# Level products of two scan directions in all quadrants, and an output projection on high and low parts

## What is computed

```python
def wkv7_scan(S0, inputs, reverse):
...
    def step(S, inp):
        r, w, k, v, kk, a = inp
        S = (S * w[:, :, None, :]
             - jnp.einsum('bhvk,bhk->bhv', S, kk)[..., None] * (kk * a)[:, :, None, :]
             + v[..., None] * k[:, :, None, :])
        return S, jnp.einsum('bhvk,bhk->bhv', S, r)
...
def odd_mixer(h_lat, h_ctx, cos, sin, w_in, w_out, sink, ctx_out):
...
    o_lat, o_ctx = window_gqa(apply_rope(q_l, cos, sin), apply_rope(k_l, cos, sin), v_l,
                              q_c, k_c, v_c, sink, ctx_out)
    return o_lat @ w_out, (o_ctx @ w_out if ctx_out else None)
```

## Time and profile before

| | |
|---|---|
| median of three runs | 2604.84 us (2599.87 to 2604.89) |
| the profiled execution | 2601.52 us, its span 2599.7 us |
| mean granted TensorE clock | 0.978 of full speed |
| TensorE, matmuls | 2442.0 us, 94% of the span |
| TensorE, loads of weights | 1989.0 us, 77% |
| VectorE | 1454.3 us, 56% |
| ScalarE | 875.5 us, 34% |
| GpSimd | 76.5 us, 3% |
| HBM, read | 307 MB, 119 GB/s over the span |
| scan | from 1099 to 1364 us |
| tail and second output projection | from 2325 to 2385 us |

### The profile page before, as it was taken

One profiled execution on the slowest core, in us unless ns is written; L12 is line 12 of the kernel. 1 busy time (PEld: TensorE's weight loads), 2 busy tenths in 40 slices (PEclk: granted clock), 3 DMA queues, 4 the chain that ended last, 5 costly groups with the idle time before them and its releaser, 6 DMA issues.

```text
span 2599.7 us, 41895 instructions
## 1 busy us (share of the span) xinstructions
PE 2442.0 (94%) x17718; PEld 1989.0 (77%) x17718; DVE 1454.3 (56%) x2326; ACT 875.5 (34%) x1491; POOL 76.5 (3%) x148
## 2 busy tenths in 40 slices
PE   8999999999999999678887999999999999999998
PEld 6687778688887767567875788877688877777997
DVE  5555565655554578666544555545655554563553
ACT  2341132422222435532224422222422222454543
POOL 0000000000000000000000000000000000000000
PEclk9999999999999999798989999999999999999999
DMA  8236526344434310000003344444344433202553
GB/s 299 99 115 218 185 98 210 138 146 135 140 138 146 132 65 33 1 3 4 4 3 130 107 144 139 137 140 145 129 138 145 136 144 125 93 33 84 190 180 130
DMA packets 55913, 310.91 MB, mean 120 GB/s; under 512 B 5936, under 2 KB 9392, under 8 KB 28080
## 3 DMA queue, kind: packets, MB, share of 16 engines
q1 hardware_dynamic: 32944, 224.75, 24.3%
q0 software_dynamic: 20736, 75.51, 8.8%
q10 hardware_dynamic: 2048, 7.98, 0.8%
HBM read 307.16 MB, written 1.05 MB: 119 GB/s over the span
## 4 chain that ended last, share of the span: by engine, by line
PEld 42%; PE 30%; issue 12%; DVE 10%; ACT 5%; PEldq 0%; DMA 0%; DVEq 0%; SPq 0%; ACTq 0%
PEld bank L1410 14%; PEld bank L1403 13%; PEld bank L1406 12%; PE bank L1252 5%; PE bank L1461 4%; PE bank L1249 2%; PE bank L1311 2%; PE bank L1327 2%; PE bank L1067 1%; PE bank L1074 1%; PE bank L1070 1%; PE bank L1139 1%; PE bank L983 1%; ACT hn L1832 1%; DVE ms L2293 1%
## 5 line engine op out<-in xcount | busy, mean ns | idle before, releaser
L2306 DVE TENSOR_TENSOR w_lo<-ring,w_hi 128x1024 fp32r<-128x1024 f32 (+1 forms) x195 | 232.5, 1192 | 441.1 <-ACT w_hi L1795 441.1
L1403 PE MATMUL bank<-ffn_x_hi,w_hi 128*128 128x512 f32 x984 | 388.7, 395 | 0.0
L1406 PE MATMUL bank<-ffn_x_lo,w_hi 128*128 128x512 f32 x984 | 388.7, 395 | 0.0
L1410 PE MATMUL bank<-ffn_x_hi,w_lo 128*128 128x512 f32 x984 | 388.7, 395 | 0.0
L1795 ACT ACTIVATE w_hi<-ring 128x1024 fp32r<-128x1024 f32 (+1 forms) x195 | 200.5, 1028 | 282.0 <-PE bank L1406 271.0
L2235 DVE SCALAR_TENSOR_TENSOR ms<-mod_rows,c_silu 128x1024 f32<-128x1024 f32 x200 | 244.0, 1220 | 1.3
L1403 PEld LDWEIGHTS bank<-ffn_x_hi,w_hi 128*128 128x128 f32 x984 | 184.4, 187 | 45.2
L1406 PEld LDWEIGHTS bank<-ffn_x_lo,w_hi 128*128 128x128 f32 x984 | 184.4, 187 | 45.2
L1410 PEld LDWEIGHTS bank<-ffn_x_hi,w_lo 128*128 128x128 f32 x984 | 184.4, 187 | 45.0
L1403 PE MATMUL bank<-ffn_h_hi,w_hi 128*128 128x512 f32 x528 | 213.4, 404 | 0.0
L1410 PE MATMUL bank<-ffn_h_hi,w_lo 128*128 128x512 f32 x528 | 208.6, 395 | 0.0
(11 more groups left out here) (456 smaller groups left out, 4580.6 us busy)
## 6 DMA issues: line engine op xcount, KB each, us to landing
ring<-in_stream SPq DMA_DIRECT2D x211, 1024.0 KB, 4.8
mod_rows<-in_mod_stream POOLq DMA_DIRECT2D x144, 512.0 KB, 3.8
one_const<-in_one ACTq DMA_DIRECT2D x1, 1665.0 KB, 14.5
mix_const<-in_two ACTq DMA_DIRECT2D x1, 1440.0 KB, 6.6
win_const<-in_win ACTq DMA_DIRECT2D x1, 1216.0 KB, 5.2
x<-in_x SPq DMA_DIRECT2D x4, 256.0 KB, 4.7
c_silu<-in_c SPq DMA_DIRECT2D x1, 1024.0 KB, 10.3
x<-in_x SPq DMA_DIRECT2D x1, 1024.0 KB, 26.8
```

The lines of the kernel that those rows point to most:

```text
L1403: mm = pe.matmul(bank[:, 0:tok], w_high, hi, start=k == 0, stop=False)
L1406: mm = pe.matmul(bank[:, 0:tok], w_high, lo, start=False, stop=False)
L1410: mm = pe.matmul(bank[:, 0:tok], w_low, hi, start=False, stop=last)
L2306: V.tensor_tensor(low[:, 0:h.nk, :], raw_half(h), high[:, 0:h.nk, :].bitcast(F32), ALU.subtract).then_inc(sem("w_split"), 1)
```

## The change

**Levels.** An inverse level is no longer two steps but single products, each of one direction: `inner` (b x m), `inverse` (mt x t1, which updates m) and `transposed` (t1 x mt, which updates mt). `inner` of one direction is issued matmul by matmul in turns with a product of the other direction: inner of direction 0 with the inverse product of direction 1 from the level before, inner of direction 1 with the inverse product of direction 0 (in the fifth level with its transposed one). The transposed products are alone, except that one. In direction 1 the matrix N has its chunks swapped between the partition halves (`swapped`), so that its two products write, or read, the other half than direction 0's: the pair stands in four quadrants of the array. A level has four steps: inner of direction 0, transposed product of direction 1 from the level before, inner of direction 1, transposed product of direction 0. The signal `level_ready` becomes two, `m_ready` and `mt_ready`, and VectorE's subtractions (`update`) wait for one bank each. A round has 9 such pairs and 10 single products.

**First products.** So that both layouts are there, the k = 0 step takes three banks (`near`, `pair`, `far`) and has five matmuls for each (g, c) in place of four; ScalarE copies for direction 1 both N transposed and its swapped form (`nt_for_b`) in one instruction, and both halves of k = 0 now stand before the first u.

**Late work.** The 30 late pieces are spread over `LATE_OVER` = 54 steps, and `OUT_FROM` moves with the number of steps from 68 to 95.

**Second projection.** `project` is dropped; `project_parts` takes the layer, with four buffers for weight parts in the second. The splits of the first four half tiles stand behind pairs 10, 11, 13 and 14 of `blend(1)`, the split of input part c behind the pair that `OUT_PARTS_AFTER` names. ScalarE's evictions of the tail signal `came_out`, which it waits for before it splits their result.

```diff
-LATE_FROM, OUT_FROM = 3, 68
+LATE_FROM, LATE_OVER, OUT_FROM = 3, 54, 95
...
-    s["project"]("w_out_2o", 1, SEQ)
+    s["project_parts"](1, SEQ)
...
+OUT_SPLIT_AFTER = 10, 11, 13, 14
+OUT_PARTS_AFTER = 13, 13, 14, 14, 15, 16, 18, 18
...
+                if layer:
+                    for n in range(4):
+                        if OUT_SPLIT_AFTER[n] == i:
+                            yield "out_weight", n
+                    for c in range(KC):
+                        if OUT_PARTS_AFTER[c] == i:
+                            yield "out_parts", c
...
+OUT_SLOTS = SPLITS, 4
...
+            return lambda n: (ph4["w_hi"][:, (n + SPLITS) % 4], ph4["w_lo"][:, (n + SPLITS) % 4])
...
+        scan[0]["nt"] = scan[0]["nt_for_b"] = idle.pop(0)
+        scan[1]["nt"], scan[1]["nt_for_b"] = rs2[:, 0, :], rs2[:, 1, :]
...
-                    for what in ("inner", "outer"):
-                        yield (what, i, lvl)
+                    yield ("inner", i, lvl, 0)
+                    if lvl > 1:
+                        yield ("outer", i, lvl - 1, 1)
+                    yield ("inner", i, lvl, 1)
+                    if lvl < LEVELS - 1:
+                        yield ("outer", i, lvl, 0)
+                yield ("outer", i, LEVELS - 1, 1)
...
+        def beside_inner(lvl, d):
+
+            if d == 0:
+                return ("inverse", 1, lvl - 1) if lvl > 1 else None
+            return ("inverse", 0, lvl) if lvl < LEVELS - 1 else ("transposed", 0, lvl)
...
-                    yield late[k - LATE_FROM]
+                while late and k >= LATE_FROM + (before - len(late)) * LATE_OVER // before:
+                    yield late.pop(0)
...
+                def small(product, h, c):
+
+
+                    bank, lhs, rhs, swapped, part = product
+                    r, col = by_head(c), by_head(h)
+                    return pe.matmul(part(bank[by_head(c ^ swapped), col]), lhs[r, col], part(rhs[r, col]), start=True, stop=True)
...
+                def product_of(kind, i, d, lvl, bank):
+
+                    way, mt = scan[d], scan[d]["mt"][i % 2]
+                    if kind == "inner":
+                        return bank, way["b"], way["m"], d, lambda t: t
+                    if kind == "inverse":
+                        return bank, mt, way["t1"], d, lambda t: blocks(t, lvl, d)
+                    return bank, way["t1"], mt, 0, lambda t: blocks(t, lvl, 1 - d)
...
+                def wait_for_outer(i, d, lvl):
+                    pe.wait_ge(sem(f"inner_ready{d}"), (LEVELS - 1) * i + lvl)
+                    pe.wait_ge(sem(f"mt_ready{d}"), LEVELS * i + lvl)
...
-                        for d in range(2):
+                        lvl, d = more
+                        beside = beside_inner(lvl, d)
+                        if beside:
+                            kind, e, at_lvl = beside
                             bank, full = take_bank()
-                            pe.wait_ge(sem(f"level_ready{d}"), LEVELS * i + lvl)
-                            small(bank, scan[d]["b"], scan[d]["m"]).then_inc(full, 1)
+                            wait_for_outer(i, e, at_lvl)
+                            second, second_full = product_of(kind, i, e, at_lvl, bank), full
+                        bank, full = take_bank()
+                        pe.wait_ge(sem(f"m_ready{d}"), (LEVELS - 1) * i + lvl)
+                        own = product_of("inner", i, d, lvl, bank)
+                        for h in range(8):
+                            for c in range(2):
+                                mm = small(own, h, c)
+                                if (h, c) == (7, 1):
+                                    mm.then_inc(full, 1)
+                                if beside:
+                                    mm = small(second, h, c)
+                                    if (h, c) == (7, 1):
+                                        mm.then_inc(second_full, 1)
...
-                        lvl, = more
-                        for d in range(2):
-                            way, mt = scan[d], scan[d]["mt"][i % 2]
-                            bank, full = take_bank()
-                            pe.wait_ge(sem(f"inner_ready{d}"), (LEVELS - 1) * i + lvl)
-                            if lvl < LEVELS - 1:
-                                small(bank, mt, way["t1"], lambda t: blocks(t, lvl, d))
-                            small(bank, way["t1"], mt, lambda t: blocks(t, lvl, 1 - d)).then_inc(full, 1)
+                        lvl, d = more
+                        bank, full = take_bank()
+                        wait_for_outer(i, d, lvl)
...
+                        if k == 0:
+                            near, pair, far = (take_bank() for _ in range(3))
+                            for g in range(4):
+                                for c in range(2):
+                                    rows = [by_head(nth ^ d) for d in range(2)]
+                                    cols = [slice(pairs[d] * P + c * C, pairs[d] * P + (c + 1) * C) for d in range(2)]
+                                    bt, kt = ([scan[d][name][rows[d], g, cols[d]] for d in range(2)] for name in ("bt", "kt"))
+                                    here, there, left, right = by_head(c), by_head(1 - c), by_head(g), by_head(4 + g)
+                                    groups = ((near, here, left, bt[0], kt[0]), (pair, here, left, bt[1], kt[1]),
+                                              (near, here, right, kt[0], bt[0]), (pair, there, right, bt[1], kt[1]),
+                                              (far, there, left, kt[1], bt[1]))
+                                    for (bank, full), to, at, lhs, rhs in groups:
+                                        mm = pe.matmul(bank[to, at], lhs, rhs, start=True, stop=True)
+                                        if (g, c) == (3, 1) and not (to is here and at is left):
+                                            mm.then_inc(full, 1)
...
+            def out_weight(layer, n):
+                if n == 0:
+                    out_used[0] = tally("w_used", KC - 1)
+                split_high(parts_out[layer], n, out_used[0], out_half(layer), 0, OUT_SLOTS[layer])
+
+            def out_high(layer, kc, tok):
+                o = (ph4 if layer else ph2)["o"]
+                nc.scalar.activation(mixed[layer]["x_hi"][:, kc, 0:tok], o[:, kc, 0:tok], ACT.Copy).then_inc(sem("o_hi_ready"), 1)
...
+            def project_parts(layer, tok):
...
                 for c in range(KC):
+                    if OUT_SLOTS[layer] <= c + OUT_SLOTS[layer] - 1 < KC:
+                        out_weight(layer, c + OUT_SLOTS[layer] - 1)
...
+                    elif what == "out_weight":
+                        out_weight(1, i)
+                    elif what == "out_parts":
+                        act.wait_ge(sem("came_out"), 2 * i + 2)
+                        out_high(1, i, SEQ)
...
+                        if u.bufs is ph4:
+                            wait_read(free)
+                            act.nop().then_inc(sem("came_out"), 1)
...
+                        if d == 0:
+                            nc.scalar.activation(way["nt"][:, cols], bank[:, 0:256], ACT.Copy).then_inc(sem("nt_ready0"), 1)
+                        else:
+                            pair = bank[:, :].rearrange("p (n t) -> p n t", n=2)
+                            nc.scalar.activation(rs2[:, :, cols], pair, ACT.Copy).then_inc(free, 1)
+                            wait_read(free)
+                            act.nop().then_inc(sem("nt_ready1"), 1)
+                            turns.next()
...
+            def out_low(layer, kc, tok):
+                if kc == 0:
+                    out_base[0] = tally("o_hi_ready", KC)
+                dve.wait_ge(sem("o_hi_ready"), out_base[0] + kc + 1)
+                o, to = (ph4 if layer else ph2)["o"], mixed[layer]
+                V.tensor_tensor(to["x_lo"][:, kc, 0:tok], o[:, kc, 0:tok], to["x_hi"][:, kc, 0:tok].bitcast(F32),
+                                ALU.subtract).then_inc(sem("o_split"), 1)
...
                 for c in range(KC):
+                    if OUT_SLOTS[layer] <= c + OUT_SLOTS[layer] - 1 < KC:
+                        split_low(parts_out[layer], c + OUT_SLOTS[layer] - 1, out_half(layer))
...
+                def update(i, kind, d, lvl):
+
+                    inverse = kind == "inverse"
+                    parity = d if inverse else 1 - d
+                    part = blocks(scan[d]["m"] if inverse else scan[d]["mt"][i % 2], lvl, parity)
+                    bank, free = full_bank()
+                    link(V.tensor_tensor(part, part, blocks(bank[:, :], lvl, parity), ALU.subtract))
+                    dve.nop().then_inc(free, 1)
+                    dve.nop().then_inc(sem(f"m_ready{d}" if inverse else f"mt_ready{d}"), 1)
...
-                                V.tensor_tensor(eight(b), eight(nt), wkv_mask(d, 1), ALU.mult)
+                                V.tensor_tensor(eight(b), eight(way["nt_for_b"]), wkv_mask(d, 1), ALU.mult)
...
 
...
```

(7 more changed lines are left out.)

178 lines of the change are left out of this document (70 added, 108 removed).

## The result

The changed kernel takes 2609.59 us in the median of 14 runs (2601.31 to 2614.58), the one before 2603.80 in 14 runs beside them. The ratio is 1.0026, 95% interval 1.0019 to 1.0032: 5 to 8 us slower. The forecast was 2583, with a range of 2568 to 2601, and 0.82 on faster. The profiled execution has a span of 2607.3 us, 7.6 more than before.

What follows compares the result with a forecast made beforehand. It took TensorE to bound the scan's levels and VectorE the head of each round, with VectorE the longer chain after the change. Scan -24.5 and projection with tail +3.8 gave -20.7 us, hence 2583 us, range 2568 to 2601.

Steps and rivals of the forecast that it cites:

- The array: Scan levels: two products on disjoint quadrants take about 0.95 us together, saving 8.6 us a round, 34 us in all.
- Rival 3: Level products: a pair does not overlap in the array; +12 to +16 us, 2618 us; chance 0.06.
- First products: Scan, k = 0 step: 1.84 us a half in place of 0.93, +1.8 us of TensorE a round, hidden in round 2.
- So the levels are TensorE's: Scan, round 2: the five levels run without a gap on TensorE, 34.3 busy of 35.0 us, so TensorE bounds them.
- VectorE as the new bound: Scan after the change: VectorE is the longer chain, with 16 us of levels a round; round 2 takes 48 us.
- hand-overs: Scan, round 2: 3.5 us added to VectorE's chain, an estimate of about 0.2 us a step.
- Rival 2: Scan: VectorE takes back most of the gain, scan gives 10 us, tail takes 4; 2598 us (2592 to 2602); chance 0.25.
- By rounds: Scan, rounds 0 to 3: -1, -9, -9 and -5.5 us, together -24.5 us.
- The tail: End of the second mixer: four hoisted weight splits cost 2.35 us each, 9.4 in all; with input parts +10.3 us.
- The projection: Second projection: 26.1 us in place of 32.6, -6.5 us.
- The sum: Whole kernel: scan -24.5 us, projection and tail together +3.8 us, total -20.7 us.

Runs made afterwards that it cites:

- scan_only: The change to the scan alone, with the old second projection, against the kernel before: ratio 1.0003 (0.9994 to 1.0013).
- partner_wide: scan_only with the second product of each pair done by 8 matmuls of 128 columns, partly wrong weights: ratio 0.9956 to the kernel before.
- scan_nomask: scan_only with VectorE's masks of b behind level 1 replaced by ones of 8 columns, so b is wrong: ratio 0.9973 to the kernel before.
- out_early: The second projection's change alone, old scan, with the tail's splits moved to earlier pairs and VectorE's parts set separately: ratio 0.9997 to the kernel before.
- dense: The kernel before with one chunk product (k = 1, first pair of chunks) done eight times in one run of 256 matmuls: its 512 records took 14.0 us.
- after: The kernel with the whole change, against the kernel before: 2609.59 us, ratio 1.0026.
- pad_real: The kernel before with an empty instruction that raises an unread semaphore behind each matmul of every level product: 2775.68 us.
- pad: The kernel before with a plain empty instruction behind each matmul of every level product; these never reached the chip: ratio 0.9996.

## Why the prediction was wrong, by its own steps

- **The array: right.** A pair was to take 0.95 us; in the rows above it took 0.96. By the Trainium skill, page "TensorEngine Tiling (Array Packing)", section "Restrictions and Gotchas", its row tiles could not write one bank at the same time; this trace again shows otherwise, 64 records in 0.96 us on two banks. Rival 3 (pairs don't overlap) is out. The busy time saved was smaller than forecast all the same: the level products kept TensorE busy for 118.3 us and now for 93.5, so 24.8 less where 34 was forecast, and the scan as a whole has 14.5 less in place of some 27.
- **First products: right.** 1.84 us a half were forecast. In round 2 both halves, 160 records, ran from 1221.57 to 1224.80, 1.6 us each.
- **"So the levels are TensorE's": the step that failed.** I read 34.3 busy of 35.0 us as work of the array, and took 9 x 0.95 us a round off it, with nothing in the sum for bringing in the instructions. The number was right and the reading wrong. A single product's 64 instructions took 0.94 us, so 256 took 3.76, and the supply brought 256 in 3.4 us at best and in 3.9 where the new levels of round 2 waited for it: the old levels already ran at about that pace, and the array's speed was no longer what to save on. In round 2, 48 us were forecast; it took 60.3, with 10.7 us of waits put down to issue (3.1 before). The pairs take no instruction away, and the first products add 64 (32 records and their loads) a round. The sign was in rows that I had: 32 records at 14.4 ns in L1515 are 1.8 us for 128, a pace that blocks 3.3 us apart can't keep up, and L1515 has 3.5 us of issue in the waits of the kernel before. I had no rival for it.
- **VectorE as the new bound: not what bound first.** The rounds were summed along VectorE, with 3.5 us for hand-overs in round 2. In the levels of that round TensorE waited for VectorE not once. In the whole scan its waits ahead of level products are 13.2 us, 9.2 of which it had before. VectorE does come next: its masks are worth 8 us in scan_only, and its waits grow when instructions get fewer (partner_wide). Rival 2 let VectorE take back most of the gain and gave 2598; the measured time lies above its range as well, and its cause is another. Even with the instructions halved, the pairs did not beat the old order.
- **By rounds.** Forecast -1, -9, -9 and -5.5 us; the trace shows 0, -2.7, +4.3 and +0.3, and +1.3 behind the fourth round, where the granted clock is 0.73 for 0.77 before. The -2.7 of round 1 is no more than two traces of the unchanged scan differ by. In all, TensorE ran at half clock for 73 us of the scan in place of 63; what that cost no run tells apart, but in the levels of round 2 the clock was full from 1237.4 to 1274.9, so there it is not the reason.
- **The tail: right.** +10.3 us were forecast, though its terms as printed add up to 10.9. The first gated sum is 13.3 us later than before and the rotation at the head of the tail 2.7, so +10.6. Two pairs begin 4.5 us apart across a split in place of 2.46 (4.8 forecast): 2330.07 and 2334.59.
- **The projection: right.** From the first to the last gated sum it was 28.8 us and is 23.1, -5.8; forecast -6.5 for the whole.
- **The sum.** -24.5 should have been +3 by the trace and +0.9 (-1.5 to +3.4) by the timed runs; +3.8 for tail and projection was +4.8 by the trace, +7.0 (4 to 10) by the timed runs.

What stays open: how the loss splits between supply and VectorE outside the levels of round 2. partner_wide gives 12 us back and scan_nomask 8, and the two overlap by an amount that no run told apart. Nor was a kernel tried in which the pairs keep their length and every instruction, with neither limit in the way, so that the 8.6 us a round of the array were never seen as time.

## What to carry to other kernels

A TensorE that is busy without a gap may be paced by its instructions: count the records of a stretch, 128 matmuls and 128 loads a block, and compare with the transfers of instructions before you put more work in parallel in the array. With small matmuls in such a stretch, what saves time is fewer of them (partner_wide); outside of one, two blocks less gave nothing that could be measured. When an order of steps gets longer, look where work that is dealt out by steps ends up. Steps hoisted from one engine to the next go where the second engine is idle (out_early).

## What the runs showed of the hardware

- Blocks of instructions (16.4 KB) start no closer than 3.3 us; matmuls that wait for nothing stop 5.3 us in 512 records (dense).
- Such stops come 125 to 128 records apart where work is dense, and end 2.3 to 2.9 us after a transfer on queue 8 has started (after, dense). They can lie in the middle of a product and are listed as issue.
- An fp32 matmul of 64 rows and 32 columns takes as long as one of 64 columns, 29 ns a record on two quadrants; at 128 columns it is 62 ns (1.00 us for 16 records).
- An empty instruction that raises a semaphore cost 98 ns between small matmuls (pad_real, with the granted clock at 0.65 in the scan), and 89 ns at full clock; one that does nothing brought no block more (pad).
